# Last stage of a hybrid attention and MoE layer: who sums the expert rows and who applies the final norm

## The reference

```python
def rmsnorm(x, g):
    xf = x.astype(jnp.float32)
    y = xf * lax.rsqrt(jnp.mean(xf * xf, axis=-1, keepdims=True) + EPS)
    return (y * g.astype(jnp.float32)).astype(x.dtype)

# end of the layer: two expert outputs per token, summed, gated by g2, added to x
x = x + g2 * hier_moe(h2, ...)
# end of the model, for context and latent tokens
y = rmsnorm(x, final_g)
```

## Time and profile before

| | us |
|---|---|
| median of 3 runs | 1052.51 (1051.99 to 1054.13) |
| profiled execution, its own time | 1052.75 |
| its span, first to last instruction | 1050.7 |
| PE / DVE / ACT / POOL busy | 916.9 / 506.2 / 413.5 / 156.7 |
| mean granted TensorE clock | 0.935 of full |

### The profile page before, as it was taken

One profiled execution on the slowest core, in us unless ns is written; L12 is line 12 of the kernel. 1 busy time (PEld: TensorE's weight loads), 2 busy tenths in 40 slices (PEclk: granted clock), 3 DMA queues, 4 the chain that ended last, 5 costly groups with the idle time before them and its releaser, 6 DMA issues. The chain is left out here.

```text
span 1050.7 us, 11939 instructions
## 1 busy us (share of the span) xinstructions
PE 916.9 (87%) x4619; PEld 693.6 (66%) x4619; DVE 506.2 (48%) x625; ACT 413.5 (39%) x568; POOL 156.7 (15%) x119
## 2 busy tenths in 40 slices
PE   3526999999999699979999974599999999999865
PEld 2315999899998455535888863477676776767532
DVE  4241313213232566644565546575656555565248
ACT  5331111101110466641334322466666656566223
POOL 0070000000000490000111000312121222322100
PEclk9757999999999699999999985699999999999988
DMA  9303532524000220020212119499999999998285
GB/s 379 131 0 123 221 120 101 209 91 144 23 21 1 91 93 2 1 68 1 81 69 72 60 50 377 149 353 365 380 360 366 363 369 360 365 368 319 73 355 196
DMA packets 39026, 190.91 MB, mean 182 GB/s; under 512 B 9654, under 2 KB 10806, under 8 KB 23992
## 3 DMA queue, kind: packets, MB, share of 16 engines
q1 hardware_dynamic: 28556, 166.56, 42.2%
q0 software_dynamic: 9216, 18.89, 4.8%
q10 hardware_dynamic: 1200, 4.72, 1.1%
HBM read 178.48 MB, written 26.35 MB: 195 GB/s over the span
## 5 line engine op out<-in xcount | busy, mean ns | idle before, releaser
L1539 DVE TENSOR_TENSOR gu_lo<-w_gu,gu_hi 128x2048 fp32r<-128x2048 f32 x64 | 146.3, 2289 | 116.0 <-ACT gu_hi L1438 115.8
L545 PE MATMUL PS<-h_hi,w_hi 128*128 128x384 f32 x432 | 147.6, 342 | 31.2 <-DVE w_lo L451 31.2
L549 PE MATMUL PS<-h_hi,w_lo 128*128 128x384 f32 x432 | 144.9, 335 | 0.0
L547 PE MATMUL PS<-h_lo,w_hi 128*128 128x384 f32 x432 | 144.9, 335 | 0.0
L1438 ACT ACTIVATE gu_hi<-w_gu 128x2048 fp32r<-128x2048 f32 x64 | 122.1, 1909 | 41.8 <-DMA w_gu<-in_w_gu 41.6
L1725 PE MATMUL PS<-gu_hi,xT_hi 128*128 128x512 f32 x256 | 115.6, 452 | 2.5 <-DVE xT_lo L1545 2.5
L1758 PE MATMUL PS<-w_d,aT 128*128 128x512 f32 x256 | 115.3, 593 | 1.2 <-ACT aT L1458 1.2
L545 PEld LDWEIGHTS PS<-h_hi,w_hi 128*128 128x128 f32 x432 | 81.6, 189 | 39.0 <-DVE w_lo L451 31.3
L1727 PE MATMUL PS<-gu_hi,xT_lo 128*128 128x512 f32 x256 | 101.3, 396 | 0.0
L1726 PE MATMUL PS<-gu_lo,xT_hi 128*128 128x512 f32 x256 | 101.0, 394 | 0.0
L1387 POOL DMA_INDIRECT y_rows<-yrows,tab x32 | 47.5, 1484 | 236.1 <-ACT yrows L1466 229.3
(11 more groups left out here) (188 smaller groups left out, 1366.5 us busy)
## 6 DMA issues: line engine op xcount, KB each, us to landing
w_gu<-in_w_gu SPq DMA_DIRECT2D x64, 1024.0 KB, 11.9
w_d<-in_w_down SPq DMA_DIRECT2D x32, 1024.0 KB, 11.2
wm<-in_w_mod SPq DMA_DIRECT2D x12, 2048.0 KB, 8.2
w_raw<-in_w_in SPq DMA_DIRECT2D x18, 512.0 KB, 8.9
yt<-y_rows SPq DMA_DIRECT2D x9, 1024.0 KB, 12.7
xt<-in_x_all SPq DMA_DIRECT2D x9, 512.0 KB, 3.4
h_rows<-h SPq DMA_DIRECT2D x9, 512.0 KB, 2.6
y_all<-yt SPq DMA_DIRECT2D x9, 512.0 KB, 2.7
```

Source lines behind the costliest of these rows:

```text
L545: pe.matmul(o, w_hi[b][:, k, :], h_hi[:, k, tok], start=k == 0, stop=False)
L547: pe.matmul(o, w_hi[b][:, k, :], h_lo[:, k, tok], start=False, stop=False)
L549: last = pe.matmul(o, w_lo[b][:, k, :], h_hi[:, k, tok], start=False, stop=k == KD - 1)
L1539: dve.tensor_tensor(gu_lo[:, n % 3, h, :], w_gu[:, n % 3, h, :], raw(gu_hi[:, n % 2, h, :]), ALU.subtract).then_inc(s_lo, 1)
```

## The change

Two tiles, 0 and 4, are no longer summed by PE: DVE adds their two rows in SBUF, then multiplies by g2 from SBUF. PE sums the other seven, in order. The last multiplication is split for tiles 0 to 7: ACT multiplies by the reciprocal root (an activation of kind Copy with a scale for each partition, in place), and POOL multiplies by `fg` (a tensor_tensor of 128x1024, in place). ACT issues scale(t-1) after the square root of tile t. Tile 8 keeps the single DVE instruction. SP still stores the tiles in order, and the last one waits on a semaphore of its own. ACT also issues one square root on a dummy column ahead of its wait for the scatters.

```diff
+        DVE_SUMS = (0, 4)
+        PE_SUMS = [t for t in range(NT) if t not in DVE_SUMS]
 # SP
-                        sp.wait_ge(s_fin, t + 1)
+                        if t < NT - 1:
+                            sp.wait_ge(s_fin, t + 1)
+                        else:
+                            sp.wait_ge(s_last, 1)
 # POOL, new
+                    pool.wait_ge(s_p7, 16)
+                    for t in range(NT - 1):
+                        pool.wait_ge(s_scaled, t + 1)
+                        pool.tensor_tensor(yt[:, t, 0, :], yt[:, t, 0, :], fg[:], ALU.mult
+                                           ).then_inc(s_fin, 1)
 # ACT
+                    act.activation(fss[:, 0, 1:2], eps_col[:], ACT.Sqrt).then_inc(s_fstd, 1)
                     for b in range(2):
                         act.wait_ge(s_out[b], 16 * NE // 2)
+                    def scale(t):
+                        act.wait_ge(s_fr, t + 1)
+                        act.activation(yt[:, t, 0, :], yt[:, t, 0, :], ACT.Copy,
+                                       scale=fss[:, t, 2:3]).then_inc(s_scaled, 1)
                     for t in range(NT):
...
                         act.wait_ge(s_fsq, t + 1)
+                        act.wait_ge(s_fstd, t + 1)
                         act.activation(fss[:, t, 1:2], fss[:, t, 0:1], ACT.Sqrt, bias=eps_col[:],
                                        scale=1.0 / D).then_inc(s_fstd, 1)
+                        if t:
+                            scale(t - 1)
 # DVE
                     def combine(t):
-                        dve.wait_ge(s_sum, t + 1)
-                        dve.tensor_tensor(halves(yt[:, t, 0, :]), PS[:, 2 * (t % 4):2 * (t % 4) + 2, :],
-                                          halves(g2row[:, t // NB, :]), ALU.mult).then_inc(s_g2, 1)
+                        out, first = halves(yt[:, t, 0, :]), halves(yt[:, t, 0, :])
+                        if t in DVE_SUMS:
+                            dve.wait_ge(s_yt[t], 16)
+                            dve.tensor_tensor(yt[:, t, 0, :], yt[:, t, 0, :], yt[:, t, 1, :],
+                                              ALU.add).then_inc(s_dsum, 1)
+                            dve.wait_ge(s_dsum, DVE_SUMS.index(t) + 1)
+                        else:
+                            dve.wait_ge(s_sum, PE_SUMS.index(t) + 1)
+                            first = PS[:, 2 * (t % 4):2 * (t % 4) + 2, :]
+                        dve.tensor_tensor(out, first, halves(g2row[:, t // NB, :]), ALU.mult
+                                          ).then_inc(s_g2, 1)
...
-                    def finish(t):
-                        dve.wait_ge(s_fstd, t + 1)
+                    def invert(t):
+                        dve.wait_ge(s_fstd, t + 2)
                         dve.reciprocal(fss[:, t, 2:3], fss[:, t, 1:2]).then_inc(s_fr, 1)
-                        dve.wait_ge(s_fr, t + 1)
-                        dve.scalar_tensor_tensor(yt[:, t, 0, :], yt[:, t, 0, :], fss[:, t, 2:3],
-                                                 fg[:], ALU.mult, ALU.mult).then_inc(s_fin, 1)
...
                         combine(t)
                         if t:
-                            finish(t - 1)
-                    finish(NT - 1)
+                            invert(t - 1)
+                    invert(NT - 1)
+                    dve.wait_ge(s_fr, NT)
+                    dve.scalar_tensor_tensor(yt[:, NT - 1, 0, :], yt[:, NT - 1, 0, :],
+                                             fss[:, NT - 1, 2:3], fg[:], ALU.mult, ALU.mult
+                                             ).then_inc(s_last, 1)
 # PE
-                    for t in range(NT):
+                    for t in PE_SUMS:
                         pe.wait_ge(s_yt[t], 16)
```

More of the change, by code:

```diff
@@ L1239, in build @@
         s_sum = sem("s_sum")
+        s_dsum = sem("s_dsum")
         s_x3 = sem("s_x3")
@@ L1243, in build @@
         s_fr = sem("s_fr")
+        s_scaled = sem("s_scaled")
         s_fin = sem("s_fin")
+        s_last = sem("s_last")
         s_store = sem("s_store")
         LAP = (NE + 2) // 3
+        DVE_SUMS = (0, 4)
+        PE_SUMS = [t for t in range(NT) if t not in DVE_SUMS]
         HALF = KD // 2 * 2 * FE
```

## The result

The changed kernel takes 1059.01 us (median of 4 runs, 1057.95 to 1060.26) against 1052.6 for the kernel before (4 runs, 1051.99 to 1054.13): ratio 1.0059, interval 1.0042 to 1.0077. Forecast were 1056.4 and a range from 1052.8 to 1058.6, so the direction was right and the size too small: 6.2 us by the ratio instead of 3.9. A second measurement beside other kernels gave 1.0049 (1.0036 to 1.0063). The profiled execution took 1057.95 us with a span of 1056.1, 5.4 us longer than before. All of the difference is in the last stage: its first tile is on chip at 1006.25, as before at 1006.33.

A forecast was written before the change was run, and what follows sets the result against it. DVE bounds the last stage at 3.79 us a tile, PE close behind at 3.42. Holds between POOL and DVE add 2.7 us and the stores 1.2: +3.9 on 1052.75, 1056.4 against the median, range 1052.8 to 1058.6.

The forecast's parts named there:

- The exclusion: Last stage: DVE instructions with two SBUF inputs and POOL's multiplications wait for each other's end, 3.34 us per tile.
- Both prices: Last stage: after the release a blocked DVE instruction costs 1.08 us, a blocked POOL one of 1024 columns 2.26.
- Rival 1: Last stage: POOL runs under DVE's adds unhindered and PE paces; 1049.1 us, faster; chance 0.11.
- The start: PE's first tile, now tile 1: loaded at 1008.7, 5.8 us with a cold clock, ready at 1014.5.
- The schedule: Last stage's queues laid out in order: last tile-wide instruction ends at 1050.3 against 1047.6, +2.7 us.
- rival 2: Last stage: PE finishes tile 1 by 1012 to 1013, POOL's work falls otherwise; 1054.1 us, same; chance 0.17.
- rival 3: Last stage: POOL holds reciprocals too, 4.9 us per tile instead of 3.34; about 1064 us; chance 0.05.
- The two stores: Kernel's end: tile 8's store follows tile 7's, which waits for POOL, adding 1.2 us.
- The end: Behind the last tile-wide instruction: the span ends 3.1 us later as before, plus 1.2 for a second store.

The follow-up runs named there:

- e_memset: The changed kernel with POOL's multiplication by final_g replaced by a memset of 2720 columns that reads nothing: ratio 0.9979 to the kernel before.
- p_last: The kernel before plus one POOL memset of 64 columns after DVE's last instruction, for which nothing waits: ratio 1.0028.
- b_nopool: The changed kernel without POOL's instruction, SP storing a tile once ACT has scaled it: ratio 0.9937 to the kernel before.
- a_tail: The changed kernel with tiles 7 and 8 both finished by DVE's single instruction, POOL stopping at tile 6: ratio 1.0019 to the kernel before.
- d_split: The changed kernel with PE summing all nine tiles, ACT and POOL keeping the split norm: ratio 1.0024 to the kernel before.

## Why the prediction was right in its direction and too small

- **The exclusion (right).** Both prices held: DVE ended 1.08 to 1.09 us after POOL, POOL 2.20 to 2.22 after DVE, where I had 2.26. Beside e_memset the holds cost 7.0 us at the last add, where my schedule had 1044.7 - 1037.9 = 6.8, and 7.4 at POOL(7), where it had 7.3. Rival 1 did not come: the add took 2.07 to 2.44 us beside a running POOL. The Trainium skill ("SBUF — State Buffer", section "Who interferes with whom") says that a GpSimd instruction that only writes does not contend with a two-input one of VectorE; the memset row agrees.
- **The start (0.66 us off).** PE's first tile was ready at 1015.16, not 1014.5. PE started at 1008.75, as forecast, but its cold pass took 6.4 us instead of 5.8. The granted clock stayed at 0.50 until about 1014.2, some 5.5 us from PE's start, where it had been 4.1 in the kernel before. I had carried the time of one cold pass over to another. Windows of the changed kernel, columns as in the earlier trace rows:

```profile
1008.75:1013.95 5.20, 5.20 (x6) 2.13 (x7) 1.23 (x1) 1.44 (x3) 0.00 (x0) 0.50 1.01 429
1013.95:1014.35 0.40, 0.40 (x2) 0.30 (x1) 0.00 (x0) 0.00 (x0) 0.00 (x0) 0.65 0.93 389
```

- **The schedule (right).** Ends forecast and measured: sum of tile 4 1027.2 and 1027.8, its multiplication 1030.5 and 1031.1, add 6 1038.0 and 1038.5, add 8 1044.7 and 1045.1, L1737 1048.1 and 1048.4, POOL(7) 1050.3 and 1050.6. The order of POOL and DVE was the forecast one at every tile, so rival 2 did not come, and reciprocals took 0.16 beside POOL, so neither did rival 3. ACT's scale was 1.13 us, not 1.06.
- **The two stores (right).** The forecast put the last landing about 3.9 us behind POOL(7); measured 1054.6 - 1050.6 = 4.0.
- **The end (the step that failed).** I took the tail of the kernel before, 3.1 us from the last tile-wide instruction to the end of the span, and added 1.2 for a second store: 4.3 us behind POOL(7). It was 5.5. The term that I had put at nothing, without a reason, is POOL's own closing: POOL was treated as an engine like DVE, done when its last instruction is done. In this block it is not. Its closing DRAIN takes 5.36 us more, against the stores' 4.0, and it set the end, 1.1 us later than the landing would have. p_last shows this by itself, b_nopool and a_tail that it goes with POOL's late work.
- **What is left.** In the profiled execution the end of the span was forecast at 1050.7 + 3.9 = 1054.6 and came at 1056.1: 0.3 us from the stage, 0.1 from the stores, 1.1 from the DRAIN. The rest is the place of the median. The forecast put it 0.24 us below the profiled execution, as in the kernel before; here it lies 1.06 above (1057.95, 1058.14, 1059.88, 1060.26). I know of no reason for it in the trace, and it is of the size by which medians of this program move: 25 and 24 more executions of the kernel before, on two chips, had medians of 1053.5 and 1054.6 against the 1052.6 here. The profiled execution, DRAIN and all, lies inside the range; without the DRAIN the median would have been inside it too. So the mechanism was right, one term was missing, and how far outside the range the median fell is in part chance.

The change as a whole: the two sums alone cost nothing that can be measured (0.9998) and the split norm alone 2.5 us, but together they cost 5 to 6. The traces put that at tile 4: there two more of DVE's instructions can be held by POOL, DVE loses 4.1 us (3.31 + 3.25 instead of 2.44), and it falls out of the phase in which d_split's adds run unheld. At the end of add 3 the changed kernel is 0.5 us ahead of d_split (+18.3 against +18.8), at the end of add 4 it is 3.9 behind (+26.1 against +22.3). No run keeps tile 0's sum on DVE and drops tile 4's, so this split of the cost is read from the traces and not tested.

## What to carry to other kernels

Before moving elementwise work from DVE to POOL, look in the trace for places where the two overlap, and count for both engines the time of all instructions that hold each other up: here a fused 1.28 us on DVE became 2.37 on POOL, and the holds cost 7.0 us by the last add. Look for the idle time of the pacing engine instead: one tuple, (0, 1, 2), gained 3.0 us in the trace and 3.6 and 4.7 by the ratios of two measurements, where the split over three engines lost 5 to 6. And look at the closing DRAIN of each engine, also where it is hidden: in the trace of the kernel before, POOL's 5.3 us were there to be read. In this block POOL's last instruction has to end some 5 us before the stores land.

## What was not expected of the hardware

- The DRAIN that closes POOL's stream in the last block takes 5.3 to 5.4 us from the end of its last instruction: 5295 ns where it starts 3.2 us behind the last scatter's instruction, 5473 under a memset of 0.15 us (p_last), 7702 under one of 2.37 (e_memset), 8158 under a multiplication of 2.80. In the earlier blocks it ends within about 0.1 us of POOL's last instruction. DVE's closing drain in the last block takes 0.04 us beyond its last instruction (1528 ns under 1490).
- A memset of 2720 columns on POOL takes 2.37 us and leaves DVE's two-input instructions at 1.21 to 1.23; a multiplication of the same 2.37 us makes the adds, the sum and the multiplication from SBUF that it holds 2.07 to 3.31.
